# Three slots and another bank layout for the dilated pair attention, head squares on ScalarE, absorbed queries and gate matmuls at other places

## The reference, cut to what matters

```python
shift, scale, res_gate = jnp.split(jax.nn.silu(c) @ w_ada + b_ada, 3, axis=-1)
h = _rms(x, norm_w) * (1 + scale[:, None]) + shift[:, None]
zq, zkv, zd, ga, gb, ma, mb = jnp.split(h @ w_in, ...)
q = (_rms(zq, qa_norm) @ w_qb).reshape(B, S, MLA_HEADS, MLA_QK)
q_nope = _rms(q[..., :MLA_NOPE], qn_g)
q_pe = _rope(_rms(q[..., MLA_NOPE:], qr_g), pos)
rows = jnp.concatenate([_rms(zkv[..., :MLA_KV_RANK], kv_norm),
                        _rope(_rms(zkv[..., MLA_KV_RANK:], kr_g), pos)], axis=-1)
dq = _rope(_rms(zd[:, :, :, 0], dq_g[:, None]), pos)
dk = _rope(_rms(zd[:, :, :, 1], dk_g[:, None]), pos)
dv = zd[:, :, :, 2]
...
# branch A: causal attention over 8 heads of 64 + 32 (rotary), keys k_nope = _rms(ckv @ w_uk)
# branch B: three dilated windows (128,1), (512,4), (2048,16), 4 heads of 64, combined by denominators
ya = (o_a * jax.nn.silu(ga)) @ w_pa
yb = (o_b * jax.nn.silu(gb)) @ w_pb
merged = jax.nn.sigmoid(ma) * ya + jax.nn.sigmoid(mb) * yb
return x + res_gate[:, None] * (merged @ w_out)
```

## Time and profile before

| what | us or share |
|---|---|
| median of three runs | 1371.1 |
| the profiled execution, whole / its span | 1372.51 / 1370.7 |
| TensorE matmuls / weight loads busy | 1219.1 (89%) / 998.1 (73%) |
| VectorE busy | 715.8 (52%) |
| ScalarE busy | 495.2 (36%) |
| GpSimd busy | 254.7 (19%) |
| chain of waits, share of span | PE 57%, DVE 19%, issue 8%, ACT 5%, DMA 5%, POOL 4% |
| read from HBM | 105.21 MB, 81 GB/s |
| mean granted clock of TensorE | 0.913 |

### The profile page before, as it was taken

The page is one execution under the profiler, slowest core; times in us unless marked ns, Lnnn a source line. Parts: engine busy times, 40 slices in busy tenths (PEclk is TensorE's granted clock), DMA queues, the critical chain, the costliest instruction groups (busy, mean ns, idle before and its releaser), DMA issues.

```text
span 1370.7 us, 22960 instructions
## 1 busy us (share of the span) xinstructions
PE 1219.1 (89%) x7616; PEld 998.1 (73%) x7616; DVE 715.8 (52%) x1657; ACT 495.2 (36%) x1159; POOL 254.7 (19%) x252
## 2 busy tenths in 40 slices
PE   5987758998897899999987999998999899997986
PEld 1277647786786678778765998988999899997431
DVE  4137887456865233030322676766676667676422
ACT  1133334332243333322322554545454545453010
POOL 0023330048865012333431000000000000000000
PEclk9989857999999657999998999999999999998579
DMA  8622010031242102233264310323232323225005
...
DMA packets 79398, 112.24 MB, mean 82 GB/s; under 512 B 8627, under 2 KB 50756, under 8 KB 79293
## 3 DMA queue, kind: packets, MB, share of 16 engines
...
HBM read 105.21 MB, written 5.68 MB: 81 GB/s over the span
## 4 chain that ended last, share of the span: by engine, by line
PE 57%; DVE 19%; issue 8%; ACT 5%; DMA 5%; POOL 4%; SPq 2%; ACTq 0%; DVEq 0%; POOLq 0%
PE ps L1376 18%; PE ps L1050 5%; PE ps L1051 5%; PE ps L1052 5%; PE ps L1357 5%; DVE ssq L2106 3%; PE ps L1065 3%; PE ps L1402 3%; DMA raw<-in_w_ada 2%; ACT cT_hi L850 2%; PE ps L1422 2%; PE ps L1212 1%; PE ps L1255 1%; POOL tmp L946 1%; PE ps L1266 1%
## 5 line engine op out<-in xcount | busy, mean ns | idle before, releaser
L931 POOL TENSOR_TENSOR wlo<-raw,whi 128x512 fp32r<-128x512 f32 (+3 forms) x148 | 172.1, 1165 | 459.8 <-ACT whi L620 459.6
L1376 PE MATMUL ps<-wq_hi,cT_hi 128*128 128x260 f32 x1024 | 217.8, 294 | 0.5 <-ACT sq L879 0.5
L1050 PE MATMUL ps<-whi,hT_hi 128*128 128x512 f32 (+3 forms) x512 | 190.3, 372 | 30.4 <-POOL wlo L931 19.2
L2106 DVE TENSOR_REDUCE ssq<-sq 128x8 f32<-128x512 f32 x256 | 172.6, 682 | 66.6 <-ACT sq L879 64.5
L1376 PE MATMUL ps<-wq_hi,cT_lo 128*128 128x260 f32 x1024 | 206.3, 283 | 0.0
L1376 PE MATMUL ps<-wq_lo,cT_hi 128*128 128x260 f32 x1024 | 206.0, 282 | 0.0
L620 ACT ACTIVATE whi<-raw 128x512 fp32r<-128x512 f32 (+3 forms) x148 | 83.3, 564 | 316.5 <-PE ps L1047 246.3
L1052 PE MATMUL ps<-whi,hT_lo 128*128 128x512 f32 (+3 forms) x512 | 185.8, 363 | 0.0
L1051 PE MATMUL ps<-wlo,hT_hi 128*128 128x512 f32 (+3 forms) x512 | 185.7, 363 | 0.0
L1376 PEld LDWEIGHTS ps<-wq_hi,cT_hi 128*128 128x128 f32 x1024 | 157.6, 190 | 1.1 <-ACT sq L879 1.1
L1376 PEld LDWEIGHTS ps<-wq_hi,cT_lo 128*128 128x128 f32 x1024 | 158.2, 189 | 0.0
...
## 6 DMA issues: line engine op xcount, KB each, us to landing
cn<-in_cache_mla SPq DMA_DIRECT2D x256, 144.0 KB, 2.1
...
```

What stands on the lines that cost most here:

```text
L931: nc.gpsimd.tensor_tensor(out=wlo[:, s % NHL, 0:width], in0=raw[:, j % NRAW, 0:width], in1=whi[:, s % NHL, 0:width].bitcast(F32), op=ALU.s ...
L1050: mm(out, hi[:, k, c], bh, start=st, stop=False)
L1376: last = mm(ps[:, 3 + 2 * (u % 2) + f, 0:260], a[c], wq[:, c, f, w], start=c == 0 and a is hi and wq is wq_hi, stop=c == 1 and a is lo)
L2106: v.tensor_reduce(out=ssq[:, (4 * g + u) * 8:(4 * g + u + 1) * 8], in_=sq4[:, u, :].rearrange("p (h e) -> p h e", e=NOPE), axis=AX, op=ALU ...
```

## The change

- **Front.** The transposes of shift and scale come after ada3, and ada4, ada5 after them. The gate item with its two matmuls moves from before Q to before TD.
- **Squares.** ScalarE now squares the heads of QB0, K and the three D QK items (`to_stage_squared`, two buffers by turns, one of them a piece of `tab`), tile by tile behind its own copy; VectorE waits for `squared` and only sums. The samples' narrow tile stays on VectorE.
- **Rotary keys.** VectorE rotates the four tiles' keys in one go; ScalarE writes them beside the K heads (`kc_rope`).
- **QB1.** VectorE takes the tiles in the order 1, 0, 3, 2, samples, and finishes 0, 2 and the samples; GpSimd finishes 1 and 3. QB0 is still GpSimd's.
- **Absorbed queries.** Their small transposes come after the latent attention, their matmuls ahead of the fourth chunk of D0QK.
- **Pair attention.** Three slots for scores, exponentials and masks (`PAIR_SLOTS`, `PAIR_AHEAD` = 2); scores have two banks each of GA's, the turn has one bank, the output is bank 7 alone. The items of GB share two banks. The transposes TE come ahead of GB's third chunk, the scores of jobs 0 and 1 ahead of its fifth.

The diff, cut to its core:

```diff
-          + [("gate", 2, "A"), ("Q", 5, "A"), ("KV", 5, "A"), ("Tq", 3, "D"), ("QB0", 5, "A"),
+          + [("Q", 5, "A"), ("KV", 5, "A"), ("Tq", 3, "D"), ("QB0", 5, "A"),
...
-STAGES += [("TD", 4 * (ND - 1), "A"), ("GA", 4, "D"), ("GAs", 1, "A"), ("TE", 4, "A"), ("GB", 4, "A"), ("GBs", 1, "A"),
+STAGES += [("gate", 2, "A"), ("TD", 4 * (ND - 1), "A"), ("GA", 4, "D"), ("GAs", 1, "A"), ("TE", 4, "A"), ("GB", 4, "A"), ("GBs", 1, "A"),
...
-_gb = [(ITEM["GB"] + t) % BANKS for t in range(BANKS)]
-PAIR_SCORES, PAIR_OUT, PAIR_TURNED = ((_gb[5], _gb[6]), (_gb[0], _gb[1])), (_gb[3], _gb[4]), (7, _gb[2])
+_ga = [(ITEM["GA"] + t) % BANKS for t in range(BANKS)]
+PAIR_SLOTS, PAIR_AHEAD = 3, 2
+PAIR_SCORES, PAIR_OUT, PAIR_TURNED = (_ga[0:2], _ga[2:4], _ga[5:7]), 7, _ga[4]
+PLACE = {ITEM["GB"] + t: (_ga[5 + t // 2], t % 2 * BW) for t in range(NT)}
+PLACE[ITEM["GBs"]] = (7, 0)
+SHARES_BANK = [ITEM["GB"], ITEM["GB"] + 2]
+HELD_BY = {ITEM["GB"] + t: ITEM["GA"] - 2 + t // 2 for t in range(NT)}
+HELD_BY[ITEM["GBs"]] = None
+for _t in range(4):
+    PLACE[ITEM["TE"] + _t], HELD_BY[ITEM["TE"] + _t] = (_ga[_t], 0), ITEM["GA"] + _t
...
+        squares = [sqt[:, :], tab[:, P + M_R16:P + M_R16 + 512]]
...
+            def to_stage_squared(idx, w):
+                k = staged[0]
+                to_stage(idx, w)
+                squared_[0] += 1
+                n = squared_[0]
+                act.wait_ge(evac_a, READER[idx][1])
+                if n > 2:
+                    act.wait_ge(square_free, n - 2)
+                nc.scalar.activation(squares[n % 2][:, 0:w], stage[:, k % NSTAGE, 0:w], ACT.Square).then_inc(squared, 1)
...
-                split_to(FIRST["GB"] + COUNT["GB"])
-                exp(0)
+                for n in range(PAIR_AHEAD):
+                    exp(n)
                 act.wait_ge(far_stored[0], 16)
                 for t in range(NT):
+                    act.wait_ge(z_done, ITEM["GB"] + t // 2 * 2 + 2)
                     copy_out(ITEM["GB"] + t, gb_of[:, t, :], BW)
                 to_stage_small(ITEM["GBs"], BW, False)
                 for n in range(len(PAIR_JOBS)):
-                    if n + 1 < len(PAIR_JOBS):
-                        exp(n + 1)
+                    if n + PAIR_AHEAD < len(PAIR_JOBS):
+                        exp(n + PAIR_AHEAD)
                     if (N_MLA_CHUNKS + n) % 2:
                         pt_copy(act, nc.scalar.activation, N_MLA_CHUNKS + n, 2 * PAIR_JOBS[n][3], pt_a, (ACT.Copy,))
...
-            for n in range(2, 6):
+            for n in range(2, 4):
                 to_stage(ITEM[f"ada{n}"], 512, n=NB + 1)
-            split_to(FIRST["Q"] + NHL)
-            for n in range(2):
-                copy_out(ITEM["gate"] + n, gate_bc[:, n * 512:(n + 1) * 512], 512)
             for k in range(KD):
                 act.wait_ge(h_f, k + 1)
                 nc.scalar.activation(hThi[:, k, :], xT[:, k, :], ACT.Copy).then_inc(h_hi, 1)
+            for n in range(4, 6):
+                to_stage(ITEM[f"ada{n}"], 512, n=NB + 1)
             for name, w in (("Q", QR), ("KV", CW)):
...
+            k0 = staged[0]
             stage_q(0)
             for c in range(2):
                 half(ITEM["Tr"] + c, rThi[:, c, :])
             for t in range(NT):
-                to_stage(ITEM["K"] + t, 512)
+                squared_[0] += 1
+                n = squared_[0]
+                if n > 2:
+                    act.wait_ge(square_free, n - 2)
+                act.wait_ge(evac_a, READER[ITEM["QB0"] + t][1])
+                nc.scalar.activation(squares[n % 2][:, 0:384], stage[:, (k0 + t) % NSTAGE, 0:384], ACT.Square)\
+                  .then_inc(squared, 1)
+            act.wait_ge(rows_ready, 4)
+            for t in range(NT):
+                nc.scalar.activation(kc[:, t, :].rearrange("p (h e) -> p h e", e=QK)[:, :, NOPE:QK],
+                                     rep(rows[:, t, KVR:CW], 1, HM), ACT.Copy).then_inc(kc_rope, 1)
+            for t in range(NT):
+                to_stage_squared(ITEM["K"] + t, 512)
             to_stage_small(ITEM["K"] + TS, 512)
             split_for("V")
...
-                    to_stage(ITEM[f"D{g}QK"] + t, 512)
+                    to_stage_squared(ITEM[f"D{g}QK"] + t, 512)
...
             mix_gates("GA", AW)
+            split_to(FIRST["GB"] + 5)
             heads_in_order(2, ITEM["TE"])
+            split_to(FIRST["GB"] + COUNT["GB"])
             pair_attention()
...
             low_to(FIRST["QB1"] + COUNT["QB1"])
             for t in range(5):
-                finish_q(t)
+                finish_q(0, t, Q_FREED + t + 1, qh0_ready, t + 1)
+            finish_q(1, 1, Q_FREED + 10 + 1, qh1_pool, 1)
+            finish_q(1, 3, Q_FREED + 10 + 3, qh1_pool, 2)
...
+            def absorbed_queries(k):
+                if k != 3:
+                    return
+                misc_begin()
+                for odd in range(2):
+                    o = 64 * odd
+                    for c in range(2):
+                        for h in range(odd, HM, 2):
+                            last = mm(ps[:, 7, c * 64 + h * NB:c * 64 + (h + 1) * NB],
+                                      wukT[o:o + 64, h // 2, c * P:(c + 1) * P],
+                                      qsT[o:o + 64, h // 2 * NB:(h // 2 + 1) * NB], start=True, stop=True)
+                    if odd == 0:
+                        last.then_inc(even_done, 1)
+                        pe.wait_ge(even_done, 1)
+                last.then_inc(misc_done, 1)
             for g in range(ND):
-                block_of(f"D{g}QK", ITEM[f"D{g}QK"], range(5), hThi, hTlo, hTs)
+                block_of(f"D{g}QK", ITEM[f"D{g}QK"], range(5), hThi, hTlo, hTs,
+                         ahead_of=absorbed_queries if g == 0 else None)
...
-            heads_turned(2, ITEM["TE"])
...
-                    if n >= 2:
-                        wait_pt(pe, c - 2)
+                    if n >= 1:
+                        wait_pt(pe, c - 1)
...
                 def first_scores(k):
-                    if k == 5:
+                    if k == 2:
+                        heads_turned(2, ITEM["TE"])
+                    elif k == 4:
                         wait_evac(pe, LAST_ITEM["TE"])
                         qk(0)
+                        qk(1)
                 block_of("GB", ITEM["GB"], range(5), hThi, hTlo, hTs, ahead_of=first_scores)
                 tr(0)
-                wait_evac(pe, ITEM["GB"] + 1)
-                qk(1)
+                wait_evac(pe, ITEM["GB"] + NT - 1)
+                qk(2)
                 wait_evac(pe, ITEM["GBs"])
                 for n, (near, i, hp, nb) in enumerate(PAIR_JOBS):
                     if n < last_job:
                         tr(n + 1)
-                    if n + 2 <= last_job:
-                        qk(n + 2)
-                    if n >= 2:
-                        pe.wait_ge(o_done, N_MLA + n - 1)
+                    if n + PAIR_SLOTS <= last_job:
+                        qk(n + PAIR_SLOTS)
+                    if n >= 1:
+                        pe.wait_ge(o_done, N_MLA + n)
...
-                kp = rows[0:n, t, KVR:CW].unsqueeze(1)
-                rotate(kp, kp, ropes[0:n, t, 128:192], 1).then_inc(rows_ready, 1)
-                dve.wait_ge(rows_ready, t + 1)
+            kp = rows[:, 0:NT, KVR:CW]
+            a4 = pe1[:, :].rearrange("p (t e) -> p t e", e=ROPE)
+            b4 = pe2[:, :].rearrange("p (t e) -> p t e", e=ROPE)
+            v.tensor_tensor(out=a4, in0=kp, in1=ropes[:, 0:NT, 128:160], op=ALU.mult)
+            v.tensor_tensor(out=b4[:, :, 0:16], in0=kp[:, :, 16:32], in1=ropes[:, 0:NT, 160:176], op=ALU.mult)
+            link(v.tensor_tensor(out=b4[:, :, 16:32], in0=kp[:, :, 0:16], in1=ropes[:, 0:NT, 176:192], op=ALU.mult))
+            v.tensor_tensor(out=kp, in0=a4, in1=b4, op=ALU.add).then_inc(rows_ready, 4)
+            dve.wait_ge(rows_ready, 4)
+            kp = rows[0:NB, TS, KVR:CW].unsqueeze(1)
...
+            def head_sums(t, z, w):
+                if t == TS:
+                    link(v.tensor_tensor(out=sqt[0:NB, 0:w], in0=z, in1=z, op=ALU.mult))
+                    return sqt[0:NB, 0:w]
+                squares_read[0] += 1
+                dve.wait_ge(squared, squares_read[0])
+                return squares[squares_read[0] % 2][:, 0:w]
...
-                for t in range(5):
+                for t in ((1, 0, 3, 2, TS) if i else range(5)):
                     q_item(i, t, zs[t])
+                if i:
+                    for n, t in enumerate((0, 2, TS)):
+                        q_finish(t, n + 1)
...
-                v.tensor_copy(out[:, :, NOPE:QK], rep(rows[0:n, t, KVR:CW], 1, HM)).then_inc(kc_ready, 1)
+                if t == TS:
+                    v.tensor_copy(out[:, :, NOPE:QK], rep(rows[0:n, t, KVR:CW], 1, HM)).then_inc(kc_ready, 1)
+                else:
+                    v.memset(flag[:, :], 0.0).then_inc(kc_ready, 1)
...
-                masks_max(0)
```

(11 more changed lines are left out.)

224 lines of the change are left out of this document (122 added, 102 removed).

## The result

| | before | changed |
|---|---|---|
| median of 12 runs, us | 1370.01 (1366.48 to 1374.36) | 1365.88 (1362.52 to 1368.63) |
| ratio, 95% interval | | 0.9969 (0.9957 to 0.9981) |
| profiled execution / span, us | 1372.51 / 1370.7 | 1364.42 / 1362.6 |
| mean granted clock | 0.913 | 0.916 |

The change makes the kernel 4.1 us faster where 15 were forecast: the sign is right and the size is not. The two profiled executions are 8.1 apart. The part of the run behind the pair attention is not a place of the change, and its length scatters too: it is 843.7 to 852.0 us in the sixteen traces of this document.

The account below looks back on a forecast made before the run. TensorE, busy 89% of the span, was taken to bound the kernel, so edits count where it waits or runs at its lower clock. Terms -5.1-1.6-2.1-19+4.2+6.3+2.3 = -15.0 gave 1357.5 us, 1356 at the median; range 1336 to 1367.

Parts of the forecast that it names:

- A: Front, up to the first projection matmul: ada4 and ada5 earlier, gate matmuls later; 5.1 us saved, 2 if the stall doubles.
- B: Rotary keys: four rotations of 0.62 us each become one of 0.9 us; 1.6 us saved.
- C: Squares of QB0 moved from VectorE to ScalarE; 2.1 us saved.
- D: From the first QB0 head to the first latent attention mask; 19 us saved, ends 15 and 24.
- the tail: From the first QB1 head to the first mask: 24.5 us was to become 10, saving 14.5.
- E: Absorbed queries return in the first dilated block, unhidden on TensorE; 4.2 us lost, 8.4 if the clock falls.
- F: Squares on ScalarE in the dilated blocks, plus gate matmuls and GA; 6.3 us lost, ends 0 and 8.
- G: Pair attention: earlier second turn gains 4.4 us, the new ring's loop loses 6.7; 2.3 us lost in all.
- Full clock in the pair attention: Rival: pair attention runs at full clock, 3.6 us per job, loop 52.8, whole 1334 us; chance 0.12.
- The ring: Rival: pair attention's new ring does not bind, copies and finishes pass in time; loop 62.6, whole 1344 us; chance 0.17.
- the lower level: Rival: latent attention starts sparser and stays at the low clock, 40 us becoming up to 80; 1397 us; chance 0.04.
- the rival of no change: Rival: pair attention's three slots do nothing, front bound elsewhere, GpSimd tiles late; 1368 to 1373 us; chance 0.05.

Follow-up runs that it names:

- e4: Changed kernel with GpSimd making D0QK's three low halves only after VectorE's third QB1 finish; first mask 185.96 us in place of 188.86, whole 1362.6 us.
- e5: Changed kernel with all QB1 finishes on VectorE and D0QK's three low halves after the fifth finish; key transposes to scores 22.4 us, whole 1358.5 us.
- e2: Changed kernel with absorbed queries and their small transposes back ahead of the latent attention; D0QK 26.11 us, whole 1376.5 us.
- e6: Changed kernel with small transposes ahead of D0QK's fourth chunk, absorbed queries ahead of D1QK's sixth; D0QK 26.92 us in place of 34.88, whole 1361.0 us.
- e3: Changed kernel with the three dilated blocks' squares back on VectorE; D0V to end of D2V 108.1 us in place of 111.8, whole 1356.5 us.
- e1: Changed kernel with pair-job copies to PT ahead of VectorE's finish and ScalarE's exponentials; pair loop 57.6 us in place of 73.5, whole 1353.1 us.
- e14: Kernel before with pair-attention scores contracting over all 128 rows, both heads mixed; pair loop 56.9 us at clock 1.00, whole 1365.3 us.

## Why the prediction was right or wrong

**Right: A, B, C.** The first projection matmul was forecast at 76.7 and was at 76.45, the medians differ by 4.6 against 5.1. With fronts that vary by 4 to 6 us the closeness is partly luck. The rotary keys gave 1.4 of 1.6. The first QB0 head came 9.1 earlier (144.15 for 153.24), of which the squares are the 2.3 that A and B leave, of 2.1.

**Wrong: D, by 4.5 us.** Up to the first QB1 head it gave 5.6 where 4.5 were forecast. The step that failed is the tail: "VectorE needs 3.3 ... and three finishes ..., so 8.0; GpSimd ... 6 to 10 ... I take 10". It took 15.6. The two engines were costed one by one, VectorE at its rows alone and only GpSimd with contention. The trace shows GpSimd near its own pace, 3.1 us for each of its two finishes, and VectorE at 13.6 us in place of 8. Three low halves that the sum did not have beside it at all account for 3.0 of the 5.6 (e4), and the two finishes handed to GpSimd, beside which VectorE took 10.6, for the other 2.6: they cost VectorE nearly what they saved (e5: 11.0 with all five finishes its own). The row that told it was among the prediction's own, the addition of 1.18 us at 132.78. The prediction read it with the Trainium skill, SBUF — State Buffer, Who interferes with whom: a VectorE instruction with two SBUF inputs contends with a GpSimd instruction that reads SBUF. The trace agrees; but the prediction put the delay on GpSimd, where the row had it on VectorE.

**Wrong: E, by 5.1 us, the largest miss.** The step that failed is the price of the queries: "At the 2.4 GHz level half of 7.22 ..." gave 4.2, "upper end 8.4, if the clock falls there". Measured 9.3 with the transposes (8.8 in D0QK and 0.5 ahead of it): 5.0 for the queries, where 3.6 were forecast, and 3.8 for 512-column matmuls at half speed behind both groups of small ones, for which the sum had no term. The end of the range had the queries at the lower clock, but not the matmuls behind them: a fall of the clock lasts beyond the work that brings it. e2 and e6 show it. Even with the smaller loss of e3, 31.7 us in D0QK, the term would be 6.2.

**Right: F in the dilated blocks,** 3.8 of 3.6, by the mechanism told (V's last tiles wait for ScalarE twice, e3). The gate and GA cost 0.7 where 2.7 were forecast: "that low half comes 6.3 later" is more than the 3.6 and 2.1 that the prediction names for it, which are 5.7. GpSimd did wait longer for it, 3.80 us for 0.91, but TensorE did not feel it: its waits in GA fell from 2.6 to 1.8.

**Right: G, 3.1 of 2.3.** The second turn gained 3.3 of 4.4, the loop lost 6.4 of 6.7. The loop's alternating 5.03 and 5.21 (forecast 5.05 and 5.3), their releasers and the 0.50 were as told, and e1 shows the cause. TensorE's own part was 0.2 too large.

**The rivals.** Full clock in the pair attention did not come (0.12), but the reason given against it, that TensorE waits more, was not what held the clock at 0.50. TensorE without waits stayed at 0.50 (e1), and TensorE at 59% busy had 1.00 (e14). The Trainium skill, TensorE: Matmul & The Clock Gate, Part 1, which has the clock follow how busy TensorE has been, does not tell these apart; the measurement decides. The ring did bind, and the latent attention took 50.4 us from its first probabilities to D0QK in place of 49.5, so it did not stay at the lower level. By its size the result is nearest to the rival of no change, but not by its way: A came, and GpSimd's tiles were not what was late. The range, 1336 to 1367, holds 1365.9 at its edge, where D's upper end and E's upper end stood; the likeliest values of both were wrong in the same direction. D, 14.5 for 19, and E, 9.3 for 4.2, miss by 9.6 us together, and the forecast is off by 10.9.
